# Fourteen filling tiles of the recurrent heads made in pairs, with seven half products a pair

## The chip, the cores and the metric

The kernel runs on one core of a Trainium2 chip. The metric is the device time of one launch in microseconds (us). Engines are PE (TensorE, matmuls), PEld (its weight loads), DVE (VectorE), ACT (ScalarE), POOL (GpSimd) and SP (SyncE, which here only issues DMAs).

## What is computed

The reference runs two transformer-like blocks over 512 tokens of width 1024, everything in float32. Only the first block's mixer matters here:

```python
h = _rmsnorm(x, norm_w[layer])
proj = jnp.einsum('bsd,de->bse', h, w_in[layer])          # ten slices of 1024 columns
(q_raw, ffwd_raw, fbwd_raw, i_raw, ga_raw,
 u_raw, v_raw, gb_raw, ma_raw, mb_raw) = jnp.split(proj, split_points, axis=-1)
y_a = _hgrn2_branch(q_raw, ffwd_raw, fbwd_raw, i_raw, ga_raw, ...)   # 8 recurrent heads, both directions
y_b = _spatial_gating_branch(u_raw, v_raw, gb_raw, ...)
```

The first five slices feed the eight recurrent heads. The slices u, v and gb (called g in the kernel) are wanted only by the stage after, the blend.

## The kernel before, in words

`gla_stage` holds the eight heads. A product of the projection is a "unit": one 128-column tile of weights against all 512 tokens, the contraction of 1024 in KT = 8 steps. A unit is a `project` (line 459): eight matmuls of 128 x 512, each with its own weight load, which the trace records as 16, two to a float32 matmul. Units go in turn to the two banks of `pj`; ACT copies each out (`evacuate`, line 580) before the bank is used again. 40 units ("p") belong to the heads, five a head, and are made one head ahead. 24 more ("v", "u", "g": `FILLS`) are filling: independent work put between the steps of a head, so that PE has something to do while DVE and ACT prepare the next step. Three of them open the stage, every head but the last takes two (`PER_HEAD`), and the last takes the remaining seven.

A head on PE (`attend`, and `attend_last` for the eighth) is an order written by hand: `turn_v`, two units, `turn_keys`, level 0, a unit, `chunk_sums`, level 1, `fill(0)`, level 2, a unit, levels 3 and 4, `fill(1)`, levels 5 to 7, a unit, `output`. A level is four 128 x 128 matmuls (line 485, eight records) on operands that DVE has scaled. On DVE the order is `operands`: for each level l it writes the exponents of level l + 1 (`level_log`, lines 742 to 745), scales the operands of level l by ACT's exponentials (`level_scale`, lines 753 to 756), and merges what PE made of level l - 2 (`merge`, lines 761 and 762). After level 4's step come `states` (lines 768 to 776) and the next head's `exponents`; after the levels come `log_sums` of the next head, the last merges and `scaled_q`. ACT's order is `decays` (the exponentials of line 616, one per level, with other work put after each by `prepare` or, in the last head, `closing`) and `out_norm`. Each engine runs its own instructions strictly in program order and waits at semaphores. `level(l)` waits for `level_scale(l)` and `merge(l - 2)`; `output` waits for all merges.

Weights lie in twelve slots of 512 KB. SP walks through the units in their order and reloads a slot when its unit is done (lines 427 to 438). The first weight tiles of the blend go to slots 4 to 9 as these come free (`BLEND_SLOTS`, line 439 on). The blend, the stage after, begins when all engines have ended the heads; it already makes its own products in pairs of tiles with the same seven half products (`product`, line 1018), with its sums of weights on DVE (lines 1243 to 1252) and its differences (line 1238).

Of the kernel before, what the change touches and what calls it, by code (L numbers as in the profile page):

```python
# [21 lines left out]
P = 128  # L22
# [39 lines left out]
for _name, _n in (("norm_w", 8), ("lb", 16), ("gnorm", 1), ("final", 8), ("mix", 8), ("pool_scale", 4),  # L62
# [8 lines left out]
FILLS = [("v", n) for n in range(4)] + [("u", 0), ("u", 1)] + [("v", n) for n in range(4, 8)] \  # L71
    + [("u", n) for n in range(2, 8)] + [("g", n) for n in range(8)]
OPENING = 3
PER_HEAD = 2
CLOSING = len(FILLS) - OPENING - PER_HEAD * (HEADS - 1)


def mixer_units():

    units = [("p", j) for j in range(QKV)] + FILLS[:OPENING]  # L80
    for i in range(HEADS - 1):
        p, f = [("p", QKV * (i + 1) + j) for j in range(QKV)], FILLS[OPENING + PER_HEAD * i:OPENING + PER_HEAD * (i + 1)]
        units += [p[0], p[1], p[2], f[0], p[3], f[1], p[4]]
    return units + FILLS[len(FILLS) - CLOSING:]

# [4 lines left out]
UG_SLOT = {("u", 0): (9, None), ("u", 1): (10, None), ("u", 2): (11, None), ("u", 3): (5, ("v", 7)), ("u", 4): (6, ("v", 7)),  # L90
# [3 lines left out]

BLEND_SLOTS = {4: ("p", QKV * HEADS - 1), 5: ("g", 2), 6: ("g", 3), 7: ("g", 4), 8: ("g", 5), 9: ("g", 6)}


def slot_value(unit):

    kind, n = unit  # L100
    if kind == "p":
        return 16 * (n // QKV + 1)
    if kind == "v":
        return 16 * (n // 4 + 1)
    slot, before = UG_SLOT[unit]
    if slot == 5:
        return 16 * (3 if before[0] == "v" else 4)
    return 16 if before is None or before[0] == "v" else 16 + slot_value(before)
# [247 lines left out]
def gla_stage(core, yaT, vg, uT, gT, raw, rs1):  # L356
# [12 lines left out]
    F_, B_, Q_, G_, V_ = range(QKV)  # L369
    scale = float(P) ** -0.5  # L370
    with ExitStack() as ctx:
# [28 lines left out]
        lnd = sb("log_diff", [P, 16])  # L400
        pj = ps("proj", [P, 2, 512])
# [3 lines left out]
        pS = ps("sum", [P, 512])  # L405
# [12 lines left out]
        h_ready = core.sem("h_ready")  # L418
        w0 = list(core.w_n)
        LEAD = 2  # L420

        with nc.Block() as block:
            @block.sync
            def _(sp):
                sp.dma_start(scan0[:], dram["scan_keep"][:]).then_inc(aux, 16)
                sp.dma_start(masks[:], dram["level_masks"][:]).then_inc(aux, 16)
                for n, (kind, m) in enumerate(UNITS):
                    if kind == "p" and m < QKV * (HEADS - 1):
                        sp.wait_ge(proj_done, n + 1)
                        j, i = m % QKV, m // QKV + 1  # L430
                        sp.dma_start(core.W[:, j, :], dram["w_gla"][i, :, j, :]).then_inc(core.w_in[j], 16)
                    if (kind, m) == ("v", 3):
                        sp.wait_ge(proj_done, n + 1)
                        sp.dma_start(core.wide(5, 4, 512), dram["w_v"][1]).then_inc(core.w_in[5], 16)
                    for (k2, m2), (slot, before) in UG_SLOT.items():
                        if before == (kind, m):
                            sp.wait_ge(proj_done, n + 1)
                            sp.dma_start(core.W[:, slot, :], dram["w_" + k2][m2]).then_inc(core.w_in[slot], 16)
                for slot in range(4, 4 + 2 * BLEND_RING):
                    sp.wait_ge(proj_done, UNIT_AT[BLEND_SLOTS[slot]] + 1)  # L440
                    blend_load(core, sp, slot - 4)

            def project(pe, unit, between=None):

                n, (kind, m) = UNIT_AT[unit], unit
                slot = m % QKV if kind == "p" else 5 if kind == "v" else UG_SLOT[unit][0]
                pe.wait_ge(core.w_in[slot], w0[slot] + slot_value(unit))
                if n >= 2:
                    pe.wait_ge(evac, n - 1)
# [12 lines left out]
            def turn_v(pe, i):  # L462
                pe.wait_ge(evac, UNIT_AT["p", i * QKV + V_] + 1)
                pe.wait_ge(st_ready, i + 1)
                for c in range(NB):
                    last = nc.tensor.transpose(pT[:, 0, c * P:(c + 1) * P], raw[:, V_, c * P:(c + 1) * P],
                                               core.ident[:])
                last.then_inc(vT_done, 1)

            def turn_keys(pe, i):  # L470
                pe.wait_ge(kd_ready, i + 1)
                pe.wait_ge(vn_ready, i + 1)
                for n in range(6):
# [38 lines left out]
            def square_sums(pe, i):  # L512
                pe.wait_ge(sq_done, i + 1)
                nc.tensor.matmul(pS[:], core.ones[:], sq[:], start=True, stop=True).then_inc(ss_done, 1)

            def attend(pe, i):
# [3 lines left out]
                def fill(n):  # L520
                    project(pe, FILLS[OPENING + PER_HEAD * i + n])
# [20 lines left out]
            def attend_last(pe, i):  # L542
                def fill(n, between=None):
                    project(pe, FILLS[len(FILLS) - CLOSING + n], between)

                turn_v(pe, i)
                fill(0, lambda: square_sums(pe, i - 1))
                fill(1)
# [15 lines left out]
                for n in range(7, CLOSING):  # L564
                    fill(n)
# [9 lines left out]
            def evacuate(act, unit):  # L575
                n, (kind, m) = UNIT_AT[unit], unit
                act.wait_ge(proj_done, n + 1)
                dst = {"p": lambda: raw[:, m % QKV], "v": lambda: vg[:, m % NB, m // NB * 512:m // NB * 512 + 512],
                       "u": lambda: uT[:, m], "g": lambda: gT[:, m]}[kind]()
                nc.scalar.copy(dst, pj[:, n % 2, :]).then_inc(evac, 1)  # L580

            def softplus(act, n, lo, chain):
# [3 lines left out]
                def first():  # L586
                    act.wait_ge(evac, UNIT_AT["p", (n - 1) * QKV + lo + 1] + 1)
# [23 lines left out]
            def decays(act, i, between):  # L611
                act.wait_ge(x_ready, i + 1)
                nc.scalar.activation(X[:], X[:], ACT.Exp).then_inc(ex_ready, 1)
                for l in range(LEVELS):
# [9 lines left out]
            def out_norm(act, i, chain):  # L624
# [3 lines left out]
                chain(nc.scalar.activation(rs[:], pS[:], ACT.Ln, bias=core.eps[:, 0:1], scale=1.0 / P))  # L628
# [3 lines left out]
            def _(act):  # L632
# [20 lines left out]
                for i in range(HEADS - 1):  # L653
# [3 lines left out]
                    def prepare(l):  # L657
# [3 lines left out]
                        if l in (1, 2, 3):  # L661
                            fb[l - 1]()
                        if l == 5:
                            evacuate(act, FILLS[OPENING + PER_HEAD * i])
# [7 lines left out]
                    evacuate(act, FILLS[OPENING + PER_HEAD * i + 1])  # L672
# [13 lines left out]
                evacuate(act, FILLS[len(FILLS) - CLOSING + 5])  # L686
                out_norm(act, HEADS - 1, chain)
                for unit in FILLS[len(FILLS) - CLOSING + 6:]:
                    evacuate(act, unit)
# [26 lines left out]

            def operands(dve, i, chain, previous, exponents_next, sums_next):

# [60 lines left out]
                level_log(0)  # L779
                if previous is not None:  # L780
                    previous()
                nc.vector.tensor_tensor(sg[:], raw[:, G_], ls[:, 3], ALU.mult)
                dve.wait_ge(ex_ready, i + 1)
                chain(nc.vector.tensor_copy(ed[:, 0], Xv[:, 0, :, P - 1]))
                chain(nc.vector.tensor_copy(ed[:, 1], Xv[:, 2, :, 0]))
                for n, (a, b) in enumerate(((qs[:], 0), (kk[:, 0], 1), (qs[:], 2), (kk[:, 1], 3))):
                    last = nc.vector.tensor_tensor(X[:, b], X[:, b], a, ALU.mult)
                last.then_inc(kd_ready, 1)
                dve.wait_ge(vT_done, i + 1)
                nc.vector.tensor_copy(vn[:].rearrange("p n c -> p (n c)"), pT[:, 0, :]).then_inc(vn_ready, 1)  # L790
                for l in range(LEVELS):
                    if l > 0:
                        dve.wait_ge(lv_ready, i * (LEVELS + 1) + l)
                    if l + 1 < LEVELS:
                        level_log(l + 1)
                    level_scale(l)
                    if l == LEVELS - 1:
                        dve.wait_ge(lv_ready, i * (LEVELS + 1) + LEVELS)
                        chain(nc.vector.tensor_copy(core.spare[:, 1:2], core.spare[:, 0:1]))
                        dve.engine_nop().then_inc(lv_ready, 1)  # L800
                    if l > 1:
                        merge(l - 2)
                    if l == 4:
                        states()
                        exponents_next()
                merge(LEVELS - 2)
                sums_next()
                for l in range(LEVELS - 1, LEVELS + 1):
                    merge(l)
# [10 lines left out]
            def _(dve):  # L820
# [34 lines left out]
                for i in range(1, HEADS - 1):  # L855
# [3 lines left out]
                    scaled_q(dve, i + 2)  # L859
                    chain.restart()  # L860
# [5 lines left out]
    for slot, times in zip(range(5, 12), (4, 2, 2, 2, 3, 3, 2)):  # L866
# [2499 lines left out]
def build(nc, dram, out):  # L3366
    with ExitStack() as ctx:
# [12 lines left out]
        with ExitStack() as first:  # L3380
# [3 lines left out]
            def opening(sp, free):  # L3384
                sp.dma_start(core.wide(5, 4, 512), dram["w_v"][0]).then_inc(core.w_in[5], 16)
                for n in range(3):
                    sp.dma_start(core.W[:, 9 + n, :], dram["w_u"][n]).then_inc(core.w_in[9 + n], 16)
# [157 lines left out]
```

## Time and profile before

| what | us |
|---|---|
| median of 3 runs (1501.77 to 1503.14) | 1503.04 |
| the profiled execution's own time | 1498.53 |
| its span in the trace | 1496.4 |
| PE busy in it | 1400.8 (94%) |
| DVE busy in it | 858.6 (57%) |
| ACT busy in it | 430.6 (29%) |
| mean granted TensorE clock | 0.983 of full |

The span is what the trace covers; the profiled execution's own time is 2.1 us longer. A row of the timeline gives start, length, engine, line, operation, what it writes and reads, the shape, a count, and in brackets how long the engine had been idle and what ended that. The length of a run of matmuls includes the end of the last one in the pipeline, so the next run starts a little before it; the pace is read from start to start.

### The profile page before, as it was taken

To read this page: it belongs to the slowest core of one execution; us is meant where nothing else is said; L and a number is where in the kernel's file an instruction comes from. 1 tells how busy PE (TensorE), PEld (TensorE's weight loads), DVE (VectorE), ACT (ScalarE), POOL (GpSimd) and SP (SyncE) were. 2 spreads that over 40 slices of the span, in tenths; PEclk is the share of its full clock that TensorE was granted. 3 is DMA by queue.
4 is the path that set the end of the run, shared out by engine and by line. 5 is a ranking of instruction groups with operands and counts; after the bars stand their busy time and mean duration, and the time that the engine had idled before them with its cause. 6 is when DMAs were issued, how large, how long until landed. Compare 5 with 4: busy or idle time off the path is not lost. (4 is left out here: it accounts for less than half of the span.)

```text
span 1496.4 us, 15038 instructions
## 1 busy us (share of the span) xinstructions
PE 1400.8 (94%) x5354; PEld 796.6 (53%) x5354; DVE 858.6 (57%) x1898; ACT 430.6 (29%) x706; POOL 57.5 (4%) x114
## 2 busy tenths in 40 slices
PE   7999999999999999999999999998899786899885
PEld 3455555555555558888888444445485433333222
DVE  5567677776777747867577349965573413222111
ACT  2435444444444415101112233134313330000000
POOL 0000000000000000000000000000000001122211
PEclk9999999999999999999999999999999996999998
DMA  7031111312210114223233122002213468999995
GB/s 290 29 113 57 42 57 30 111 57 57 70 42 15 43 57 169 85 68 103 88 139 135 38 84 71 15 9 85 77 65 147 152 265 341 400 409 405 407 409 164
DMA packets 38970, 201.97 MB, mean 135 GB/s; under 512 B 6896, under 2 KB 8816, under 8 KB 32112
## 3 DMA queue, kind: packets, MB, share of 16 engines
q1 hardware_dynamic: 31600, 186.29, 33.2%
q0 software_dynamic: 4608, 8.40, 2.3%
q10 hardware_dynamic: 2688, 6.29, 1.1%
q8 instruction: 46, 0.75, 0.2%
q14 instruction: 28, 0.23, 0.0%
HBM read 196.77 MB, written 12.58 MB: 140 GB/s over the span
## 5 line engine op out<-in xcount | busy, mean ns | idle before, releaser
L459 PE MATMUL gla_proj<-hT,weight_slots 128*128 128x512 f32 x864 | 379.5, 592 | 1.9 <-DVE hT L825 1.9
L459 PEld LDWEIGHTS gla_proj<-hT,weight_slots 128*128 128x128 f32 x864 | 160.8, 190 | 188.3 <-issue 187.6
L3102 PE MATMUL moe_banks<-weight_slots,moe_room 128*64 128x512 f32 x400 | 93.4, 616 | 14.3 <-DMA weight_slots<-in_w_gu 11.7
L1847 PE MATMUL mid_p_proj<-hT,weight_slots 128*128 128x512 f32 x208 | 93.0, 595 | 1.8 <-PEq L171 1.8
L3258 DVE SCALAR_TENSOR_TENSOR moe_room<-moe_banks,moe_kept,moe_room 128x256 f32<-128x256 f32 x16 | 7.7, 484 | 128.7 <-ACT moe_room L3213 128.7
L616 ACT ACTIVATE gla_level_decay<-gla_level_decay 128x1024 f32<-128x1024 f32 x56 | 58.9, 1055 | 46.0 <-DVE gla_level_decay L745 45.5
L1847 PEld LDWEIGHTS mid_p_proj<-hT,weight_slots 128*128 128x128 f32 x208 | 39.1, 190 | 52.1 <-issue 52.1
L3102 PEld LDWEIGHTS moe_banks<-weight_slots,moe_room 128*64 128x64 f32 x400 | 29.4, 141 | 69.9 <-issue 55.0
L485 PEld LDWEIGHTS gla_level<-gla_level_q,gla_level_k 128*128 128x128 f32 x448 | 55.0, 192 | 11.5 <-issue 11.5
L580 ACT COPY gla_raw<-gla_proj 128x512 f32<-128x512 f32 x38 | 22.4, 590 | 122.9 <-PE gla_proj L459 122.9
L485 PE MATMUL gla_level<-gla_level_q,gla_level_k 128*128 128x128 f32 x448 | 56.3, 275 | 0.0
L459 PE MATMUL gla_proj<-weight_slots,hT 128*128 128x512 f32 x128 | 55.9, 592 | 0.0
L3213 ACT ACTIVATE moe_room<-moe_banks,moe_kept 128x256 f32<-128x256 f32 x16 | 7.6, 474 | 160.1 <-PE moe_banks L3102 160.1
L761 DVE COPY spare<-spare 128x1 f32<-128x1 f32 x64 | 9.5, 149 | 71.8 <-PE gla_level L485 71.3
L2800 POOL DMA_INDIRECT ex_rows<-h_rows,ix_rows x1 | 1.2, 1196 | 1248.4 <-issue 1248.4
L762 DVE COPY_PREDICATED gla_scores<-gla_level_masks,gla_level 128x512 f32<-128x512 int32 x64 | 46.8, 731 | 2.2
L3127 PE MATMUL moe_banks<-weight_slots,moe_room 128*64 128x512 f32 x176 | 41.7, 619 | 4.1 <-issue 4.1
L459 PEld LDWEIGHTS gla_proj<-weight_slots,hT 128*128 128x128 f32 x128 | 23.9, 190 | 28.2 <-issue 28.2
L3268 DVE COPY moe_room<-moe_banks 128x512 f32<-128x512 f32 x16 | 11.1, 692 | 48.6 <-PE moe_banks L3127 48.6
L2514 DVE CUSTOM_DVE_ANT_0 sa_probs<-sa_S,qkT_bias 128x512 f32<-128x512 f32 (+3 forms) x32 | 14.4, 489 | 39.8 <-PE sa_S L2317 39.8
L753 DVE TENSOR_TENSOR gla_level_q<-gla_q,gla_level_decay 128x256 f32<-128x256 f32 x56 | 23.4, 417 | 16.2 <-ACT gla_level_decay L616 16.2
L1018 PE MATMUL bl_p_x<-hT,weight_slots 128*128 128x256 f32 x128 | 30.0, 380 | 1.9 <-PEq L171 1.9
(503 smaller groups left out, 2483.3 us busy)
## 6 DMA issues: line engine op xcount, KB each, us to landing
weight_slots<-in_w_gu SPq DMA_DIRECT2D x25, 2048.0 KB, 22.0
weight_slots<-in_w_gla SPq DMA_DIRECT2D x40, 512.0 KB, 3.6
weight_slots<-in_w_dn SPq DMA_DIRECT2D x10, 2048.0 KB, 28.0
weight_slots<-in_w_merge SPq DMA_DIRECT2D x32, 512.0 KB, 4.2
weight_slots<-in_w_out SPq DMA_DIRECT2D x16, 512.0 KB, 4.5
weight_slots<-in_w_v SPq DMA_DIRECT2D x3, 2048.0 KB, 7.5
hT<-in_w_gu SPq DMA_DIRECT2D x3, 2048.0 KB, 36.0
weight_slots<-in_w_u SPq DMA_DIRECT2D x8, 512.0 KB, 5.6
```

The costliest lines, as they stand in the source:

```text
L459: last = nc.tensor.matmul(pj[:, n % 2, :], lhsT, rhs, start=(k == 0), stop=(k == KT - 1))
L485: last = nc.tensor.matmul(pA[:, l % 2, c * P:(c + 1) * P], k, q, start=True, stop=True)
L580: nc.scalar.copy(dst, pj[:, n % 2, :]).then_inc(evac, 1)
L616: nc.scalar.activation(Tl[:, l % 2], Tl[:, l % 2], ACT.Exp).then_inc(e_ready, 1)
L753: nc.vector.tensor_tensor(side(QL[:, l % RING], 0), side(qs[:], 0), side(Tl[:, l % 2, 1], 0), ALU.mult)
L762: nc.vector.copy_predicated(A[:], masks[:, l].unsqueeze(1).to_broadcast([P, NB, P]), pA[:, l % 2].rearrange("p (n t) -> p n t", t=P)).then ...
L1018: ins = nc.tensor.matmul(bank, b[:, k * P:(k + 1) * P], a[:, k, :], start=first and k == 0, stop=(k == H - 1), skip_group_check=not first)
L1847: last = nc.tensor.matmul(pw[:, n % 2, :], a, b, start=(k == 0), stop=(k == KT - 1))
L2514: last = nc.vector.tensor_tensor_reduce(pr[:, i % RINGP, hh, 0:w], pS[:, i % 2, hh, 0:w], bias[:, b, 0:w], 1.0, -3.0e38, ALU.add, ALU.max, ...
L3102: last = nc.tensor.matmul(pG[rows, e, :], hgT[:, k, rows], core.as_gate_up(at[k // 4])[:, x, k % 4, :], start=(k == 0), stop=(k == KT - 1))
L3127: last = nc.tensor.matmul(pY[rows, half, :], hidT[:, e, f * P + CAP * x:f * P + CAP * x + CAP], core.as_down(at)[:, x, f, half * 512:half ...
L3268: nc.vector.tensor_copy(ys[:, e, 512:1024], pY[:, 1, :]).then_inc(yb, 1)
```

## The change

The tiles u1 to u7 and g0 to g6 are made two at a time. Written as 2 x 2 blocks of half the contraction by 128 columns of weights (b11, b21 from the first tile, b12, b22 from the second) and half the contraction by 256 tokens of hT, the eight half products of a pair become seven, each four matmuls of 128 x 256. "x" of a pair (`pair_opens`) makes x first, z first, x second, z second; "y" (`pair_closes`) makes y first, z third, y second. Heads 3 to 6 take one pair each, x at `fill(0)` and y at `fill(1)`. The last takes three pairs and g7. The four combinations of hT (`form`) are made once, into slots 5 to 8; four sums of weights (`weight_sums`) and five differences (`second`, `third`, `rest_22`, `rest_21`, `rest_12`) are made on DVE for each pair, two copies on ACT in place of two. The bank `pZ` takes the place of `pS`, which now is half of `pT`. Slots 9 and 10 carry the pairs, one after another (the sixth pair is in slots 11 and 4), and the blend's slots 5 to 9 are loaded after ("y", 6).

```diff
+FIRST_PAIRED = 3
+PAIRED = [(("u", 1), ("u", 2)), (("u", 3), ("u", 4)), (("u", 5), ("u", 6)), (("u", 7), ("g", 0)), (("g", 1), ("g", 2)),
+          (("g", 3), ("g", 4)), (("g", 5), ("g", 6))]
+PAIR_SLOTS = [(9, 10)] * 5 + [(11, 4), (9, 10)]
-BLEND_SLOTS = {4: ("p", QKV * HEADS - 1), 5: ("g", 2), 6: ("g", 3), 7: ("g", 4), 8: ("g", 5), 9: ("g", 6)}
+BLEND_SLOTS = {4: ("y", 5), 5: ("y", 6), 6: ("y", 6), 7: ("y", 6), 8: ("y", 6), 9: ("y", 6)}
...
+            def product(bank, b, a, first, between=None):
+                for k in range(H):
+                    if k == 1 and between is not None:
+                        between()
+                    ins = nc.tensor.matmul(bank, b[:, k * P:(k + 1) * P], a[:, k, :], start=first and k == 0,
+                                           stop=(k == H - 1), skip_group_check=not first)
+                return ins
+            def pair_opens(pe, n, between=None):
...
+                product(bank, b11(n), hT[:, 0:H, 0:Q], True, between).then_inc(xa_done, 1)
+                pe.wait_ge(formed, 2)
+                pe.wait_ge(summed, 4 * n + 2)
+                if n:
+                    pe.wait_ge(c21_out, n)
+                product(pZ[:, 0:Q], sums[:, 1], forms[:, 1], True).then_inc(z1_done, 1)
+                pe.wait_ge(x1_out, n + 1)
+                product(bank, b21(n), hT[:, H:KT, 0:Q], False).then_inc(proj_done, 1)
...
+                pe.wait_ge(u2_out, n + 1)
+                product(pZ[:, 0:Q], b12(n), forms[:, 2], False).then_inc(z2_done, 1)
+            def z_third(pe, n):
+                pe.wait_ge(summed, 4 * n + 4)
+                pe.wait_ge(u3_out, n + 1)
...
+            def y_second(pe, n):
+                pe.wait_ge(formed, 4)
+                pe.wait_ge(c22_out, n + 1)
...
             def attend_last(pe, i):
                 turn_v(pe, i)
-                fill(0, lambda: square_sums(pe, i - 1))
-                fill(1)
+                pair_opens(pe, 4, lambda: square_sums(pe, i - 1))
+                pair_closes(pe, 4)
                 turn_keys(pe, i)
                 level(pe, i, 0)
                 chunk_sums(pe, i)
-                fill(2)
+                pair_opens(pe, 5)
                 level(pe, i, 1)
+                pair_closes(pe, 5)
                 level(pe, i, 2)
-                fill(3)
                 level(pe, i, 3)
+                pair_opens(pe, 6)
                 level(pe, i, 4)
-                fill(4)
-                for l in range(5, LEVELS + 1):
-                    level(pe, i, l)
-                fill(5)
+                y_first(pe, 6)
+                level(pe, i, 5)
+                z_third(pe, 6)
+                level(pe, i, 6)
+                y_second(pe, 6)
+                level(pe, i, 7)
                 output(pe, i)
-                fill(6, lambda: square_sums(pe, i))
-                for n in range(7, CLOSING):
-                    fill(n)
+                project(pe, LAST_PLAIN, lambda: square_sums(pe, i))
...
                 def closing(l):
-                    if l in (0, 1, 3, 5, 6):
-                        evacuate(act, FILLS[len(FILLS) - CLOSING + (0, 1, 3, 5, 6).index(l)])
+                    if l == 1:
+                        x_first_out(act, 5)
+                    if l == 2:
+                        evacuate(act, ("x", 5))
+                    if l == 4:
+                        x_first_out(act, 6)
+                    if l == 5:
+                        evacuate(act, ("x", 6))
...
+            def weight_sums(dve, n):
...
+                nc.vector.tensor_tensor(sums[:, 0], b11(n), b12(n), ALU.add).then_inc(summed, 1)
+                dve.wait_ge(summed, 4 * n + 1)
+                nc.vector.tensor_tensor(sums[:, 1], sums[:, 0], b22(n), ALU.add).then_inc(summed, 1)
...
                 for l in range(LEVELS):
                     if l > 0:
                         dve.wait_ge(lv_ready, i * (LEVELS + 1) + l)
                     if l + 1 < LEVELS:
                         level_log(l + 1)
+                    if n == 0 and l == 2:
+                        form(dve, 2)
+                    if last_head and l == 2:
+                        second(dve, 5)
                     level_scale(l)
+                    if last_head and l == 0:
+                        rest_12(dve, 4)
+                        weight_sums(dve, 5)
...
+                    if n == 0 and l == 3:
+                        form(dve, 3)
+                    if n == -1 and l == 4:
+                        weight_sums(dve, 0)
+                    if paired and l == 4:
+                        second(dve, n)
+                        third(dve, n)
+                    if last_head and l == 3:
+                        third(dve, 5)
+                    if last_head and l == 4:
+                        rest_22(dve, 5)
+                    if last_head and l == 5:
+                        rest_12(dve, 5)
+                    if last_head and l == 6:
+                        second(dve, 6)
                     if l > 1:
                         merge(l - 2)
                     if l == 4:
                         states()
                         exponents_next()
+                    if paired and l == 5:
+                        rest_22(dve, n)
+                    if last_head and l == 4:
+                        rest_21(dve, 5)
+                    if last_head and l == 5:
+                        weight_sums(dve, 6)
```

What the diff above leaves out: in heads 3 to 6 DVE makes `rest_21` and `rest_12` after the levels, before `merge` 5, and the next pair's `weight_sums` after `scaled_q`; at the end of head 2 it makes `form` 0 and 1. ACT makes `x_first_out` after the exponential of level 4 and no copy for y. In the last head DVE makes `second` 4 after the first `level_log`, `third` 4 before it waits for ACT's edge exponentials, `rest_22` and `rest_21` 4 around the copy of v, `third` and `rest_22` 6 after the levels; ACT makes `x_first_out` 4 and `evacuate` ("x", 4) around the edge exponentials, before the first level's. `turn_keys` also waits for `rs_done` of the head before.

## Rows read from the trace of the kernel before

**Rows 1.** The page: busy time of each engine over the whole span.
```profile
PE 1400.8 (94%) x5354; PEld 796.6 (53%) x5354; DVE 858.6 (57%) x1898; ACT 430.6 (29%) x706; POOL 57.5 (4%) x114
```

**Rows 2.** Stretches (head 4, last): length; PE, PEld, DVE, ACT, POOL busy; PEclk; DMA.
```profile
313.90:375.68 61.78, 61.24 (x222) 33.42 (x221) 46.13 (x108) 27.14 (x32) 0.00 (x0) 1.00 0.21 60
499.25:561.87 62.62, 62.36 (x224) 33.69 (x222) 38.31 (x100) 16.79 (x22) 0.00 (x0) 1.00 0.14 44
```

**Rows 3.** Timeline of PE, head 4.
```profile
339.58 7.03 PE L459 MATMUL gla_proj<-hT,weight_slots 128*128 128x512 f32 x16
346.45 1.05 PE L485 MATMUL gla_level<-gla_level_q,gla_level_k 128*128 128x128 f32 x8
...
365.99 7.03 PE L459 MATMUL gla_proj<-hT,weight_slots 128*128 128x512 f32 x16
373.35 0.49 PE L503 MATMUL gla_out<-gla_scores,gla_v 128*128 128x128 f32 x2 [0.33 <-DVE gla_scores L762]
```

**Rows 4.** Timeline of PE at the start of the blend.
```profile
568.98 1.89 PE L1018 MATMUL bl_p_z<-bl_h_forms,bl_w_sums 128*128 128x256 f32 x8
570.70 1.89 PE L1018 MATMUL bl_p_y<-hT,bl_w_sums 128*128 128x256 f32 x8
```

**Rows 5.** Timeline of DVE at the start of the blend: a form, a difference, a sum.
```profile
566.24 1.22 DVE L1238 TENSOR_TENSOR bl_h_forms<-hT 128x1024 f32<-128x1024 f32 x1
...
571.01 0.41 DVE L1238 TENSOR_TENSOR bl_second<-bl_first,bl_p_z 128x256 f32<-128x256 f32 x1
571.34 0.68 DVE L1243 TENSOR_TENSOR bl_w_sums<-weight_slots 128x512 f32<-128x512 f32 x1
```

**Rows 6.** Timeline of DVE, head 4.
```profile
340.60 0.41 DVE L742 TENSOR_TENSOR gla_level_decay<-gla_cum 128x256 f32<-128x256 f32 x1
...
342.94 0.41 DVE L756 TENSOR_TENSOR gla_level_k<-gla_keys,gla_level_decay 128x256 f32<-128x256 f32 x1
347.54 0.15 DVE L761 COPY spare<-spare 128x1 f32<-128x1 f32 x1 [4.19 <-PE gla_level L485]
...
357.49 0.74 DVE L762 COPY_PREDICATED gla_scores<-gla_level_masks,gla_level 128x512 f32<-128x512 int32 x1
...
375.88 0.43 DVE L725 COPY gla_edge<-gla_cum 128x512 f32<-128x512 f32 x1 [2.02 <-PE gla_out L505]
```

**Rows 7.** Timeline of ACT: two rows of head 4, one of the blend.
```profile
338.99 1.05 ACT L616 ACTIVATE gla_level_decay<-gla_level_decay 128x1024 f32<-128x1024 f32 x1
...
363.06 0.59 ACT L580 COPY xT<-gla_proj 128x512 f32<-128x512 f32 x1 [2.79 <-PE gla_proj L459]
...
565.72 0.37 ACT L1147 COPY bl_first<-bl_p_x 128x256 f32<-128x256 f32 x1 [3.23 <-PE bl_p_x L1018]
```

**Rows 8.** Timeline of PE, last head.
```profile
524.36 1.95 PE L485 MATMUL gla_level<-gla_level_q,gla_level_k 128*128 128x128 f32 x16
```

**Rows 9.** Timeline of DVE, last head.
```profile
525.45 0.15 DVE L761 COPY spare<-spare 128x1 f32<-128x1 f32 x1 [3.06 <-PE gla_level L485]
...
529.75 0.28 DVE L768 COPY gla_states<-gla_turned 128x128 f32<-128x128 f32 x1
...
531.80 0.42 DVE L742 TENSOR_TENSOR gla_level_decay<-gla_cum 128x256 f32<-128x256 f32 x1
```

**Rows 10.** Busy time by stretch, late stage (columns as in rows 2).
```profile
1304.00:1308.00 4.00, 3.93 (x14) 2.34 (x16) 1.36 (x3) 0.00 (x0) 0.00 (x0) 0.50 1.02 396
1308.00:1312.00 4.00, 4.00 (x18) 1.14 (x16) 0.81 (x2) 0.59 (x1) 0.23 (x2) 0.87 1.04 438
```

**Rows 11.** Timeline of PE, late stages.
```profile
1145.56 3.67 PE L2099 MATMUL cr_p_q<-hT,weight_slots 128*128 128x512 f32 x8 [2.08 <-PEq L1541]
...
1304.07 1.97 PE L3089 MATMUL moe_banks<-ident,ex_rows 128*128 128x128 f32 x8 [4.15 <-DMA ex_rows<-h_rows,ex_ix]
...
1420.53 5.35 PE L3102 MATMUL moe_banks<-weight_slots,moe_room 128*64 128x512 f32 x16 [2.10 <-DMA weight_slots<-in_w_gu]
```

**Rows 12.** DMA issues, 360 to 376 us: size in KB, us to landing.
```profile
weight_slots<-in_w_gla SPq DMA_DIRECT2D x1, 512.0 KB, 3.6
```

More of the change, by code:

```diff
@@ L104, in slot_value @@
         return 16 * (n // 4 + 1)
[L105 to L108, printed above, removed]
+    return 16 if unit == ("u", 0) else 48
 PLACES = 11
@@ L400, in gla_stage @@
         lnd = sb("log_diff", [P, 16])
+        sums = sb("w_sums", [P, 3, H * P])
+        forms = flat(core.W[:, 5:9, :]).rearrange("p (n k t) -> p n k t", n=4, t=Q)
         pj = ps("proj", [P, 2, 512])
@@ L404, in gla_stage @@
         pO = ps("out", [P, 512])
-        pS = ps("sum", [P, 512])
+        pZ = ps("pair", [P, 512])
+        pS = pT[:, 1, :]
         aux = core.sem("aux_loaded")
@@ L434, in _ @@
                         sp.dma_start(core.wide(5, 4, 512), dram["w_v"][1]).then_inc(core.w_in[5], 16)
[L435 to L438, printed above, removed]
+                    if (kind, m) in (("u", 0), ("p", QKV * HEADS - 1)):
+                        sp.wait_ge(proj_done, n + 1)
+                        pair_load(sp, 5, int(kind == "p"))
+                    if kind == "y" and m < len(PAIRED) - 1:
+                        sp.wait_ge(proj_done, n + 1)
+                        if m == 5:
+                            sp.dma_start(core.W[:, 11, :], dram["w_g"][7]).then_inc(core.w_in[11], 16)
+                        else:
+                            for x in range(2):
+                                pair_load(sp, m + 1 if m < 4 else 6, x)
                 for slot in range(4, 4 + 2 * BLEND_RING):
@@ L577, in evacuate @@
                 act.wait_ge(proj_done, n + 1)
+                if kind == "x":
+                    nc.scalar.copy(part(m, 0, 0), pj[:, n % 2, 0:Q]).then_inc(evac, 1)
+                    return
                 dst = {"p": lambda: raw[:, m % QKV], "v": lambda: vg[:, m % NB, m // NB * 512:m // NB * 512 + 512],
@@ new lines, in form, with second @@
+            def form(dve, n):
+                if n == 0:
+                    dve.wait_ge(proj_done, UNIT_AT["v", 7] + 1)
+                    sub(forms[:, 0], hT[:, 0:H, Q:T], hT[:, H:KT, Q:T]).then_inc(formed, 1)
+                    return
+                dve.wait_ge(formed, min(n, 2))
+                a, b = ((hT[:, 0:H, 0:Q], forms[:, 0]), (hT[:, H:KT, Q:T], forms[:, 1]), (hT[:, H:KT, 0:Q], forms[:, 1]))[n - 1]
+                sub(forms[:, n], a, b).then_inc(formed, 1)
+            def second(dve, n):
+                dve.wait_ge(x1_out, n + 1)
+                dve.wait_ge(z1_done, n + 1)
+                sub(part(n, 0, 1), part(n, 1, 0), pZ[:, 0:Q]).then_inc(u2_out, 1)
@@ new lines, in third, with rest_22, rest_21 @@
+            def third(dve, n):
+                dve.wait_ge(z2_done, n + 1)
+                sub(part(n, 1, 1), part(n, 1, 0), pZ[:, 0:Q]).then_inc(u3_out, 1)
+            def rest_22(dve, n):
+                dve.wait_ge(y1_done, n + 1)
+                dve.wait_ge(u3_out, n + 1)
+                sub(part(n, 1, 1), pj[:, UNIT_AT["y", n] % 2, 0:Q], part(n, 1, 1)).then_inc(c22_out, 1)
+            def rest_21(dve, n):
+                dve.wait_ge(z3_done, n + 1)
+                sub(part(n, 1, 0), part(n, 1, 0), pZ[:, 0:Q]).then_inc(c21_out, 1)
@@ L717, in operands, with rest_12 @@
+            def rest_12(dve, n):
+                dve.wait_ge(proj_done, UNIT_AT["y", n] + 1)
+                dve.wait_ge(u2_out, n + 1)
+                sub(part(n, 0, 1), pj[:, UNIT_AT["y", n] % 2, 0:Q], part(n, 0, 1)).then_inc(c12_out, 1)
             def operands(dve, i, chain, previous, exponents_next, sums_next):
+                n, last_head = i - FIRST_PAIRED, i == HEADS - 1
+                paired = n >= 0 and not last_head
                 if previous is not None:
@@ L805, in operands @@
                         exponents_next()
+                    if paired and l == 5:
[4 more added lines that the diff above has]
+                        weight_sums(dve, 6)
+                if paired:
+                    rest_21(dve, n)
+                    rest_12(dve, n)
+                if last_head:
+                    third(dve, 6)
+                    rest_22(dve, 6)
                 merge(LEVELS - 2)
                 sums_next()
-                for l in range(LEVELS - 1, LEVELS + 1):
-                    merge(l)
+                if last_head:
+                    rest_21(dve, 6)
+                merge(LEVELS - 1)
+                if last_head:
+                    rest_12(dve, 6)
+                merge(LEVELS)
             def result(dve, i, chain, h):
@@ L865, in gla_stage @@
         core.w_n[j] += 16 * HEADS
-    for slot, times in zip(range(5, 12), (4, 2, 2, 2, 3, 3, 2)):
+    for slot, times in zip((4, 5, 9, 10, 11), (1, 2, 6, 6, 3)):
         core.w_n[slot] += 16 * times
```

139 lines of the change are left out of this document (114 added, 25 removed), and 3 rows, old and new, of the table UG_SLOT.

## The prediction

> **What bounds the kernel now.** I read the page first: PE is busy for 94% of the span [rows 1]. Then the eight heads, where the change lies: in head 4 PE is busy for 61.24 of 61.78 us at full clock while DVE is busy for 46.1, in the last head for 62.36 of 62.62 with DVE at 38.3 [rows 2]. So PE sets the length of a head and what shortens its matmuls shortens the kernel, as long as DVE's and ACT's new work fits their idle time at the right moment. Third, the timelines, for when each engine reaches each step.
>
> **PE's saving.** A unit takes 6.87 us, start to start (339.58 to 346.45), and the next starts at once [rows 3]. A pair is now two units, 13.73 us. Each of the seven half products is eight records of 128 x 256, which the blend makes in 1.72 us, start to start [rows 4]; seven are 12.04 us. A pair saves 1.7 us: "x" takes 6.9, as the unit it replaces, "y" 5.15. Seven pairs would give 12 us if nothing waited.
>
> Against this speaks a rule. The blend's row shows 24 more weight loads a pair (56 for 32) at no cost: its records stand exactly half as far apart as those of 512 columns [rows 3, 4]. The Trainium skill ("TensorE: Matmul & The Clock Gate", Back-to-back issue gap) says that the spacing in a stream of loads and matmuls is set by both, and that at few columns the matmul's own time counts too little; its "LDWEIGHTS" section gives 107 ns a load. By an estimate from that page, 24 exposed loads would cost 2.6 us a pair and make each pair 0.9 us slower.
>
> **New work on DVE and ACT.** A weight sum takes 0.6 to 0.7 us, a difference 0.35 to 0.4, a form 1.2 [rows 5]; per pair four sums (2.6 us) and five differences (1.8 us). ACT copies 256 columns in 0.37 instead of 512 in 0.59 [rows 7]. The bound for the new waits on pZ comes from the same rows: it is the blend's own operation.
>
> **Heads 3 to 6: the work fits.** Head 4, in the times of before. x first starts at 339.58 [rows 3], ends at 341.3, z first at 343.0. ACT has ended the exponential of level 4 at 340.0 [rows 7] and copies x first by 341.9, 1.1 us before x second wants it. DVE ends level 4's scaling at 343.3 [rows 6] and makes `second` by 343.7; z second wants it at 344.7. `third` waits for z second until 346.7, inside the 4.2 us in which DVE stood idle for level 2 [rows 6]. y first starts where `fill(1)` did, 6.87 us before its end at 362.86 (ACT's copy follows at 363.06 [rows 7]), so at 356.0, and z third ends at 359.4; DVE ends merge 3 at 358.2 [rows 6] and `rest_22` by 358.6, so y second has some 0.6 us to spare, the tightest place. `weight_sums` of the next pair (2.5 us) falls where DVE waits for `output` (2.0 us [rows 6], and more now). Its two loads are issued nearly ten microseconds earlier, against 3.6 us to landing [rows 12]. The forms go into head 2's end (2.4 us against 2.0 idle; PE asks for DVE's work there only at `turn_keys`, two units or 13.7 us later) and into idle time of head 3, the first pair's sums into level 4's wait of head 2: nothing.
>
> There is a second gain. Now ACT can start the next head's log-sigmoid only after copying `fill(1)` at 363.06 [rows 7], and DVE's `log_sums` and last merges follow from it; PE's `output` starts at 373.35 instead of 372.86, with a slow first step, some 0.55 us in all [rows 3]. y needs no copy by ACT, so this chain starts 3 us earlier and the wait goes. Per head 1.7 + 0.55 = 2.3 us, four heads: 9.2 us saved.
>
> **The last head: the work does not fit.** Three pairs come in one head, and the order on DVE is fixed. A level costs DVE 2.7 us (`level_log` and `level_scale`, 340.60 to 343.3 [rows 6]), a merge 0.8, `states` 2.05 (529.75 to 531.80 [rows 9]), two levels on PE 1.78 (524.36 + 1.95, less the overlap of 0.17 [rows 8]). Counting us from `turn_v`, and each engine in its order:
> - y second of pair 4 wants `rest_22` at 11.6, DVE has it at 12.0: 0.4 wait.
> - Level 0 wants its operands at 14.4. DVE has them at 15.6, since two differences, a wait for z second and `rest_21` stand before: 1.2.
> - z third of pair 5 wants `third` at 27.4, it ends at 28.1 after level 3's scaling: 0.8.
> - y second of pair 5 wants `rest_22` at 29.9, but it stands behind level_log 5, scaling 4 and merge 1: 31.9. Wait 2.1.
> - Levels 2 and 3 end at 35.5, x first of pair 6 at 37.2. z first then wants `weight_sums(6)`. DVE had been waiting for level 2 (34.6) and has, in order, merge 2 (0.85), `states` with its waits (2.2), `rest_21`, level_log 6 and scaling 5 (2.7), `rest_12`, merge 3 (0.85) and two sums (1.4): they are there at 43.5. Wait **6.3**.
> - x second ends at 46.95. ACT's exponential of level 6 stands behind its copy of x, so it ends at 48.5; scaling 6 (1.4) and `second(6)` follow: z second starts at 50.6. Wait 3.7.
> - At the end `third`, `rest_22`, `rest_21` and `rest_12` stand between the merges, and `output` waits 1.2.
>
> Together 15.7 us of waits, less three savings of 1.7 and the 0.4 that PE waits there now: the last head becomes 10.1 us longer. The same working for the kernel of before gives 61.8 us for a head and 62.2 for the last, against 61.8 and 62.6 read [rows 2].
>
> **The clock.** In these heads the granted clock is 1.0, 2.4 GHz [rows 2]. After an idle 4.15 us in a late stage it was 0.5 (1.2 GHz) for the 4 us that follow and 0.87 over the next 4 [rows 10, 11], about 2.5 us lost; after one of 2.10 us sixteen records took 5.35 us, which at 0.22 each would be 3.5, about 1.8 lost; after another of 2.08 us nothing was lost (eight took 3.67, at 0.43 each 3.4 and the end of the last) [rows 11]. The waits of 6.3 and 3.7 us are of the kind that loses it, and z first and x second of pair 6 between them are on the chain. Bounds: 0 (clock held) and 5 us (both falls in full). I take 2.7: one fall in full, as after the 4.15 us, and little of the second.
>
> **After the head.** y6 ends 12 us before the blend can begin (level 7, `output`, g7 and the 1.85 us of the stage's end), so the five loads behind it land in time at 3.6 us the first: nothing, at most 2 us if they queue.
>
> **Sum.** -9.2 + 10.1 + 2.7 = +3.6 us, on the profiled execution's 1498.53 us: 1502.1. That execution lies 4.5 us under the median; I put the same +3.6 on the median, 1503.04, and get 1506.6. From no change this kernel's measurement can tell about 0.2%, 3.0 us.
>
> **Rivals.**
> 1. The clock holds or hardly falls: +0.9 us, 1503.9. For it: waits of 2 us passed without loss [rows 11]. Against: 6.3 us is three times as long.
> 2. DVE gets ahead in the last head. If its idle 3.1 us before merge 1 [rows 9] and the rest absorb the work, and `weight_sums(6)` is there when z first wants it, the last head saves its 5.2 us: -9.2 - 5.2 = -14.4, 1488.7; with half of the waits (7.8 us) -6.5, 1496.5. It decides on whether the two sums are there before x first ends, at 37.2. Against: the sums stand after merge 3 in DVE's program, and merge 3 after level 3 on PE, so at least 2.2 us must pass where x first covers 1.7, before `states` and level 6 are counted.
> 3. The pairs stall in heads 3 to 6 as well, at y second, where 0.6 us is spare, or at `second`: from 0.6 us of lateness on it costs. If DVE is 2.1 us later than I have it (three differences and a merge that I have placed wrongly), 1.5 us show in each of four heads, +6: +9.6, 1512.6. For it: the margin is thin. Against: DVE's steps there are read, not assumed [rows 6].
> 4. The loads of weights are exposed (the page's rule as a mechanism of this kernel): the blend's half product would have to take longer here than its 1.72 us. A record of a level, 128 columns and a load, takes 0.11 us (16 in 1.78 [rows 8]); if each of the 24 extra loads showed that much, it costs 2.6 us a pair, 18 us in seven: +22, 1525. The blend's rows speak against it outright [rows 4].
>
> **Chances.** Forecast (waits as worked out, with a fall of the clock) 0.54, between +1.5 and +6.5. Rival 1: 0.12. Rival 2: 0.14, nearly all in its weaker form. Rival 3: 0.18. Rival 4: 0.02. Faster by over 0.2% is rival 2, 0.14. Slower by over 0.2% is rivals 3 and 4 and over half of the forecast's case, 0.50. The rest, 0.36, is within 0.2%: rival 1 and the lower part of the forecast. The range leaves out the strong end of rival 2 and the outer part of rival 3: 1498.5 to 1512.0.
>
> **What would show it.** In the profile after: head starts (`turn_v`) 59.5 us apart from head 3 on; rows of the product's line in the heads, 32 records of 128 x 256 in x, in 6.9 us; PE's wait for DVE's weight sums before the first product of pair 6, near 6 us, and one of over 3 us for the difference after it; the granted clock under 1 in the last 35 us of the heads; last head near 75 us. I am wrong if the last head is under 66 us, if PE waits at the pairs of heads 3 to 6, or if a half product there takes over 1.8 us.

## The result, and the profile after

The changed kernel takes 1504.95 us (median of 11 runs, 1502.26 to 1508.16) against 1502.13 (11 runs of before). The ratio is 1.0023, with a 95% interval of 1.0013 to 1.0034: by this ratio 3.5 us slower, between 2 and 5 (the two medians alone are 2.8 us apart). The forecast was +3.6 us; as a time it was 1506.6, put on the earlier median of 1503.04. In the profiled execution, 1504.95 us:

```profile
span 1503.2 us, 15499 instructions
PE 1395.2 (93%) x5522; PEld 831.0 (55%) x5522; DVE 894.0 (59%) x1965; ACT 427.5 (28%) x706; POOL 57.3 (4%) x114
```

PE is busy for 5.6 us less than in [rows 1] and DVE for 35 us more, and the whole is longer. So PE has less to do and stands more. Where it stands is shown by the busy time of the changed kernel in two stretches, head 6 but for its first 0.45 us, and the last head up to the blend's first product (length; PE, PEld, DVE, ACT, POOL busy; granted clock; DMA share; GB/s):

```profile
431.00:490.09 59.09, 58.87 (x242) 37.60 (x241) 50.29 (x117) 26.46 (x32) 0.00 (x0) 1.00 0.07 24
490.09:568.32 78.23, 62.21 (x296) 49.48 (x295) 48.81 (x124) 16.05 (x23) 0.00 (x0) 0.93 0.18 65
```

Head 6 is as full as head 4 was before [rows 2], with DVE at 50.3 us instead of 46.1. The last head has 16 us in which PE does nothing, and a granted clock of 0.93. The starts of heads 3, 4, 5 and 6 (`turn_v`, timeline of PE) stand 59.54 us apart, where they were 61.78 before:

```profile
251.91 0.60 PE L573 MATMUL gla_turned<-ident,gla_raw 128*128 128x128 f32 x4
311.46 0.60 PE L573 MATMUL gla_turned<-ident,gla_raw 128*128 128x128 f32 x4
371.00 0.60 PE L573 MATMUL gla_turned<-ident,gla_raw 128*128 128x128 f32 x4
430.55 0.60 PE L573 MATMUL gla_turned<-ident,gla_raw 128*128 128x128 f32 x4
```

The last head begins at 490.09 instead of 499.25: 9.2 us gained. The blend begins at 568.32 instead of 563.72, 4.6 us late. So the last head takes 78.2 us instead of 64.5, and gives back 13.8. (0.2 of the 9.2 us is no gain of the pairs: the changed kernel's first head already starts at 67.42 instead of 67.62.) This is where (timeline of PE, last head, after):

```profile
502.30 1.97 PE L507 MATMUL gla_proj<-weight_slots 128*128 128x256 f32 x8 [0.30 <-DVE weight_slots L848]
...
505.82 1.16 PE L594 MATMUL gla_level<-gla_level_q,gla_level_k 128*128 128x128 f32 x8 [0.90 <-DVE gla_level_k L938]
...
518.41 1.97 PE L507 MATMUL gla_pair<-hT,gla_w_sums 128*128 128x256 f32 x8 [0.56 <-DVE weight_slots L848]
522.23 1.97 PE L507 MATMUL gla_proj<-weight_slots 128*128 128x256 f32 x8 [1.85 <-DVE weight_slots L848]
524.03 1.95 PE L594 MATMUL gla_level<-gla_level_q,gla_level_k 128*128 128x128 f32 x16
525.81 1.89 PE L507 MATMUL gla_proj<-hT,weight_slots 128*128 128x256 f32 x8
533.63 3.75 PE L507 MATMUL gla_pair<-weight_slots,gla_w_sums 128*128 128x256 f32 x8 [5.93 <-DVE gla_w_sums L858]
537.18 1.98 PE L507 MATMUL gla_proj<-hT,weight_slots 128*128 128x256 f32 x8
542.92 2.54 PE L507 MATMUL gla_pair<-weight_slots 128*128 128x256 f32 x8 [3.77 <-DVE weight_slots L848]
545.26 1.91 PE L594 MATMUL gla_level<-gla_level_q,gla_level_k 128*128 128x128 f32 x8
...
556.30 0.49 PE L612 MATMUL gla_out<-gla_scores,gla_v 128*128 128x128 f32 x2 [1.00 <-DVE gla_scores L944]
```

These are the seven waits of the prediction, in its order and at its places: 0.3, 0.9, 0.56, 1.85, 5.93, 3.77, 1.0, together 14.3 us. The brackets count from the modelled end of the last matmul, the prediction from when the next one would have started. Counted its way (at z first of pair 6 from 525.81 + 1.73 to 533.63: 6.1 us) the seven are 0.5, 1.1, 0.7, 2.0, 6.1, 3.9 and 1.2, together 15.5 where 15.7 were forecast. After the longest, z first of pair 6 takes 3.55 us from start to start, not 1.73. The granted clock has fallen to 0.50, its lower level of 1.2 GHz, and it falls again after the next wait, of 3.77 us (stretches of z first of pair 6 and of level 4, columns as above):

```profile
533.63:537.18 3.55, 3.55 (x9) 2.83 (x9) 1.11 (x2) 0.00 (x0) 0.00 (x0) 0.50 0.02 5
545.26:546.97 1.71, 1.71 (x9) 1.71 (x8) 0.00 (x0) 0.00 (x0) 0.00 (x0) 0.50 0.00 0
```

What DVE does in PE's 5.9 us (timeline of DVE, after):

```profile
525.12 0.15 DVE L943 COPY spare<-spare 128x1 f32<-128x1 f32 x1 [3.04 <-PE gla_level L594]
...
527.99 0.41 DVE L848 TENSOR_TENSOR weight_slots<-weight_slots,gla_pair 128x256 f32<-128x256 f32 x1
528.32 0.42 DVE L924 TENSOR_TENSOR gla_level_decay<-gla_cum 128x256 f32<-128x256 f32 x1
...
531.51 0.72 DVE L944 COPY_PREDICATED gla_scores<-gla_level_masks,gla_level 128x512 f32<-128x512 int32 x1
532.13 0.68 DVE L856 TENSOR_TENSOR gla_w_sums<-weight_slots 128x512 f32<-128x512 f32 x1
532.84 0.69 DVE L858 TENSOR_TENSOR gla_w_sums<-gla_w_sums,weight_slots 128x512 f32<-128x512 f32 x1
...
540.62 0.43 DVE L935 TENSOR_TENSOR gla_level_q<-gla_q,gla_level_decay 128x256 f32<-128x256 f32 x1 [5.88 <-ACT gla_level_decay L738]
```

DVE first stands idle for 3.0 us, waiting for level 2; then come merge 2, the states, `rest_21`, level 6's exponents, level 5's scaling, `rest_12`, merge 3, and only then the two sums that PE wants. The last row is the cause of the 3.8 us: DVE waits 5.9 us for ACT's exponential of level 6. In the timeline of ACT:

```profile
528.01 1.06 ACT L738 ACTIVATE gla_level_decay<-gla_level_decay 128x1024 f32<-128x1024 f32 x1
539.19 0.37 ACT L692 COPY weight_slots<-gla_proj 128x256 f32<-128x256 f32 x1 [10.12 <-PE gla_proj L507]
539.46 1.06 ACT L738 ACTIVATE gla_level_decay<-gla_level_decay 128x1024 f32<-128x1024 f32 x1
```

ACT stood for 10.1 us at its copy of x, with the exponential queued behind it.

### The profile page after: what moved, and what is told of

It reads as the page before. It is cut to its first block and busy times, and to the rows that moved or that the text cites. A ratio compares the mean times of both kernels' runs of the same rounds, so it can differ in the third digit from the quotient of the medians.

```text
span 1503.2 us, 15499 instructions
## 1 busy us (share of the span) xinstructions
PE 1395.2 (93%) x5522; PEld 831.0 (55%) x5522; DVE 894.0 (59%) x1965; ACT 427.5 (28%) x706; POOL 57.3 (4%) x114
## 5 line engine op out<-in xcount | busy, mean ns | idle before, releaser
L566 PE MATMUL gla_proj<-hT,weight_slots 128*128 128x512 f32 x640 | 281.0, 592 | 1.9 <-DVE hT L1053 1.9
L566 PEld LDWEIGHTS gla_proj<-hT,weight_slots 128*128 128x128 f32 x640 | 119.2, 190 | 141.0 <-issue 140.2
```

Source lines behind the costliest of these rows:

```text
L566: last = nc.tensor.matmul(pj[:, n % 2, :], lhsT, rhs, start=(k == 0), stop=(k == KT - 1))
```

## The experiments

In each of them the length of the last head is taken from `turn_v` to the blend's first product, in one profiled execution. Each ratio is to runs of the kernel before that were made beside it. The changed kernel (1.0023) was not run again beside the experiments, so a difference from it in ratio goes over two such comparisons.

**1. The sums earlier.** One move on DVE in the last head.

```diff
                     if last_head and l == 4:
                         rest_22(dve, 5)
+                        weight_sums(dve, 6)
...
-                    if last_head and l == 5:
-                        weight_sums(dve, 6)
```

> One edit on the changed kernel: in the last head DVE makes weight_sums(6) straight after rest_22(5), in the 3.0 us in which it waits for level 2, not behind merge 3. Theory (the order on DVE makes PE's wait of 5.9 us): that wait falls to at most 1.2 us (z first then waits for rest_21(5), which still stands behind states), the clock does not fall there, and the last head, 78.2 us from turn_v to the blend's first product, becomes 70 to 71.5 us; against the kernel of before about -3 us, ratio 0.998. The wait of 3.8 us for second(6) stays, since ACT's copy of x and the exponential of level 6 still stand before it. Rival (DVE simply has too much work in this head, wherever it stands): the wait only moves, to level 4 or to the next product, and the last head stays over 76 us, ratio over 1.001.

Measured: ratio 0.9990 (0.9979 to 1.0001), last head 71.30 us (489.96 to 561.26), granted clock in it 0.98. Timeline of PE of this experiment:

```profile
528.40 1.97 PE L507 MATMUL gla_pair<-weight_slots,gla_w_sums 128*128 128x256 f32 x8 [0.84 <-DVE weight_slots L848]
...
535.86 2.72 PE L507 MATMUL gla_pair<-weight_slots 128*128 128x256 f32 x8 [3.77 <-DVE weight_slots L848]
```

The wait of 5.93 us has become 0.84, now for `rest_21(5)`, and z first of pair 6 runs at full pace. The wait of 3.77 us is unchanged and now it alone is followed by a lower clock (0.70 granted from 535.86 to 538.50). The last head is 6.9 us shorter than in the changed kernel. The rival, that DVE has too much work wherever it stands, falls: DVE had idle time at the place to which the sums were moved. By the traces this experiment shows it; its ratio holds 1.000.

**2. PE kept at work in its two long waits.**

```diff
+            def warm(pe, count):
+                pe.wait_ge(y_done, HEADS)
+                for k in range(count):
+                    nc.tensor.matmul(pO[:], core.ones[:], hT[:, k, :], start=True, stop=True)
...
+                if n == 6:
+                    warm(pe, 6)
                 pe.wait_ge(formed, 2)
                 pe.wait_ge(summed, 4 * n + 2)
...
+                if n == 6:
+                    warm(pe, 3)
                 pe.wait_ge(formed, 3)
```

> One edit on the changed kernel: before its two long waits in pair 6 PE makes dummy products of 128 x 512 into the idle bank of the output, six (5.2 us) in the wait of 5.9 us and three (2.6 us) in that of 3.8 us. The order and the waits of DVE and ACT are untouched. Theory (the lost clock costs some 3.6 us on top of the waits): granted clock 1.00 throughout the heads, z first of pair 6 back from 3.55 to 1.73 us, last head 78.2 -> 74.5 to 75 us, ratio to before about 1.000. Rival (the clock is no cost of its own, since DVE and ACT set the pace after these waits anyway): clock back at 1.00 but the last head within 1 us of 78.2, ratio 1.002.

The dummy products go to the bank of the output, which is idle then. Measured: ratio 1.0007 (0.9995 to 1.0019), last head 74.74 us. Timeline of PE, and the stretch of the last head, of this experiment:

```profile
528.01 5.31 PE L514 MATMUL gla_out<-hT,ones 128*128 128x512 f32 x12
534.11 1.97 PE L507 MATMUL gla_pair<-weight_slots,gla_w_sums 128*128 128x256 f32 x8 [0.79 <-issue]
...
537.64 2.74 PE L514 MATMUL gla_out<-hT,ones 128*128 128x512 f32 x6
541.57 1.97 PE L507 MATMUL gla_pair<-weight_slots 128*128 128x256 f32 x8 [1.19 <-DVE weight_slots L857]
```
```profile
490.57:565.31 74.74, 66.44 (x314) 50.19 (x313) 48.80 (x124) 16.05 (x23) 0.00 (x0) 1.00 0.20 69
```

PE does more work than in the changed kernel and the stretch is 3.5 us shorter, at a granted clock of 1.00. The waits themselves are as they were: z first begins 6.1 us after x first has ended (528.01 to 534.11), as in the changed kernel (527.5 to 533.63). (The row's "issue" names no releaser; DVE's second sum ends at 534.00, just before.) The rival, that the clock costs nothing since DVE and ACT set the pace, falls in the trace; the ratio alone, whose interval holds 1.000 and overlaps that of the changed kernel, would not decide it. So of the 13.8 us that the last head lost, 3.5 are the clock and 10.3 the waits less the saving. The changed kernel's own rows give 3.6: z first and x second of pair 6 are 1.9 us longer than at full clock, z second 0.6, level 4 0.8 and y first 0.3.

**3. The last head plain.** Pairs in heads 3 to 6 alone; g1 to g7 in the last head in the order of before, with their weights in slots of their own as these come free.

```diff
-LAST_PLAIN = ("g", 7)
+LAST = [("g", n) for n in range(1, 8)]
+LAST_SLOTS = {1: (9, ("y", 3), 5), 2: (10, ("y", 3), 5), 3: (11, ("u", 0), 2), 4: (5, ("y", 3), 3), 5: (6, ("y", 3), 1), 6: (7, ("y", 3), 1),
+              7: (10, ("g", 2), 6)}
```

> The change without its last head: pairs in heads 3 to 6 alone, the last head with seven plain tiles (g1 to g7) in the order of before. Theory (the gain of the pairs in heads 3 to 6 is 9.2 us and whole, all that is lost is in the last head): last head 64.5 us as before, kernel -9.2 us, ratio 0.9939. Rival (the earlier start is partly given back later, at loads of the blend or in the last stages): ratio over 0.996.

Measured: ratio 0.9936 (0.9919 to 0.9952), -9.6 us. The last head runs from 490.89 to 555.22, 64.3 us. PE's waits from head 3 to the blend, all of them (engine, line, for whom, total us, times, longest):

```profile
PE bl_p_x L1206 <- PEq L189: 1.7, 1, 1.7
PE gla_level L592 <- DVE gla_scores L931: 1.1, 5, 0.2
```

The wait before `output` is gone in heads 3 to 6. Their gain is whole, and by the runs nothing after it takes it back. All that the change lost it lost in the last head.

**4. Two more moves.** On the first experiment, `rest_21(5)` before merge 2 too, and `second(6)` before the scaling of level 6.

```diff
                         weight_sums(dve, 6)
+                        rest_21(dve, 5)
...
+                    if last_head and l == 6:
+                        second(dve, 6)
                     level_scale(l)
...
-                    if last_head and l == 6:
-                        second(dve, 6)
```

> On the first experiment, two more moves on DVE in the last head: rest_21(5) also before merge 2, and second(6) before the scaling of level 6 (so not behind ACT's exponential of level 6). Theory (each wait has one cause, the order): waits before z first of pair 6 gone, before z second of pair 6 from 3.8 to about 1.5 us, clock 1.00 in the heads, last head 66 to 66.5 us, against before -7.4 us, ratio 0.995. Rival (DVE's whole load binds): last head over 70 us.

Measured: ratio 0.9958 (0.9943 to 0.9972), last head 66.16 us (490.46 to 556.62). Timeline of PE of this experiment:

```profile
527.90 1.89 PE L507 MATMUL gla_pair<-weight_slots,gla_w_sums 128*128 128x256 f32 x8
532.72 1.97 PE L507 MATMUL gla_pair<-weight_slots 128*128 128x256 f32 x8 [1.20 <-DVE weight_slots L848]
```

The two waits of 9.7 us together are 1.2, by three moves of instructions that DVE makes in any case. With all seven pairs the kernel is now 6.3 us faster than before. In the traces its last head is still 1.8 us longer than in the third experiment, 66.16 against 64.33, though the intervals of the two ratios overlap: the remaining waits of this head (0.3, 0.9, 0.56, 1.85, 1.2, 1.0) are more than its three pairs save (5.2 us).

**5. One pair in the last head, where DVE is idle.** Heads 3 to 6 as in the change; in the last head g1 to g4 and g7 plain, the pair (g5, g6) with x after level 4 and y after level 7.

```diff
                 level(pe, i, 4)
+                pair_opens(pe, 4)
                 for l in range(5, LEVELS + 1):
                     level(pe, i, l)
+                pair_closes(pe, 4)
                 output(pe, i)
...
+                if last_head:
+                    second(dve, 4)
+                    third(dve, 4)
                 merge(LEVELS - 2)
...
                 merge(LEVELS)
+                if last_head:
+                    rest_22(dve, 4)
+                    rest_21(dve, 4)
+                    rest_12(dve, 4)
```

> Pairs in heads 3 to 6, and in the last head one pair alone, (g5, g6), where the trace shows DVE idle: x after level 4, y after level 7 and before the output; g1 to g4 and g7 are plain tiles. Its differences stand before merge 5 (DVE idle for 4.9 us there) and after the last merge. Theory (a pair saves 1.7 us wherever DVE reaches its steps in time): no wait of PE over 0.3 us in the last head, 62.6 to 63.0 us from turn_v to the blend's first product against 64.5, ratio to before 0.9927 (-10.9 us), 1.7 us less than with the last head plain. Rival (the last pair ends too near the end of the stage: the blend's weights in slots 5 to 9 are loaded only after it, or the differences after the last merge are late): PE waits at y second or at the blend's start, last head 64.5 us or more, ratio 0.994.

Measured: ratio 0.9931 (0.9916 to 0.9946), -10.4 us, the lowest ratio of all versions. The last head is 62.68 us. Timeline of PE of this experiment:

```profile
535.54 1.13 PE L591 MATMUL gla_level<-gla_q,gla_level_k 128*128 128x128 f32 x8 [0.21 <-DVE gla_scores L932]
536.51 1.89 PE L504 MATMUL gla_proj<-weight_slots,gla_w_sums 128*128 128x256 f32 x8
538.24 1.89 PE L504 MATMUL gla_pair<-hT,gla_w_sums 128*128 128x256 f32 x8
539.96 1.89 PE L504 MATMUL gla_proj<-weight_slots 128*128 128x256 f32 x8
541.69 0.38 PE L609 MATMUL gla_out<-gla_scores,gla_v 128*128 128x128 f32 x2
...
553.61 5.42 PE L1214 MATMUL bl_p_x<-hT,weight_slots 128*128 128x256 f32 x24 [1.70 <-PEq L188]
```

No wait between the products, none at the blend's start beyond its usual 1.7 us. The traces give 1.65 us less for the last head than with it plain; the two ratios (0.9936, 0.9931) are too close for the runs to tell them apart.

**6. The margin in heads 3 to 6.**

```diff
-                    if paired and l == 5:
-                        rest_22(dve, n)
...
+                    if paired and l == 6:
+                        rest_22(dve, n)
```

> One edit on the changed kernel: in heads 3 to 6 DVE makes rest_22 only after the scaling of level 6, about 1.6 us later; the last head is left as it is. This measures the margin that my third rival was about. Theory (y second has 0.6 to 0.9 us to spare in these heads, read from DVE's difference, ended at 415.7, and y second, begun at 416.6): PE waits 0.7 to 1.1 us at y second in each of the four heads, heads 60.3 to 60.6 us apart instead of 59.54, kernel +3 to +4.4 us on the changed one, ratio to before 1.0045 to 1.005. Rival (the delay is taken up by the waits that follow on levels 5 to 7, which PE had anyway): heads within 0.3 us of 59.54, ratio 1.0023.

Measured: ratio 1.0049 (1.0033 to 1.0065), heads 60.6 us apart. Timeline of PE of this experiment:

```profile
312.35 0.60 PE L573 MATMUL gla_turned<-ident,gla_raw 128*128 128x128 f32 x4
...
358.92 1.97 PE L507 MATMUL gla_proj<-weight_slots 128*128 128x256 f32 x8 [0.82 <-DVE xT L848]
...
372.96 0.60 PE L573 MATMUL gla_turned<-ident,gla_raw 128*128 128x128 f32 x4
```

`rest_22` in the changed kernel (head 5, timeline of DVE), and in this experiment (head 4):

```profile
415.26 0.41 DVE L848 TENSOR_TENSOR xT<-gla_proj,xT 128x256 f32<-128x256 f32 x1
```
```profile
358.35 0.42 DVE L848 TENSOR_TENSOR xT<-gla_proj,xT 128x256 f32<-128x256 f32 x1
```

Counted from y first (413.13 and 354.49) it begins 2.1 and 3.9 us in, a delay of 1.7 us. It costs PE 0.82 us of waiting and 1.06 us of each head. In the changed kernel the difference ends at 415.67 and y second begins at 416.59; here 0.15 us lie between the two (358.77 to 358.92). So y second has nearly 0.8 us to spare where 0.6 were forecast, and the other 1.0 of the 1.7 us is paid in full: my third rival was a real mechanism, some 0.8 us away from costing anything.

## Why the prediction was right, point by point

- **Seven half products at 1.72 us.** Right: 398.41 to 400.14 is one of many. The third experiment gives the whole gain of four heads, so the weight loads are not exposed. The fourth rival is refuted in these heads as in the blend. So is the estimate of 2.6 us more a pair from the Trainium skill ("TensorE: Matmul & The Clock Gate", Back-to-back issue gap and LDWEIGHTS).
- **Heads 3 to 6.** -9.2 forecast; from head 3's start to the last head's it is 238.18 us instead of 247.13, so -8.95. Per head 2.24: the pair's 1.7 and the 0.55 of the wait before the output, which is gone (481.0 + 6.87 = 487.86, the output's start). The prediction had rounded the same two terms up to 2.3.
- **The waits of the last head.** +10.1 forecast; with the clock held it is 74.74 - 64.47 = +10.3. Each wait was found at its place, within 0.3 us counted the prediction's way, and z first of pair 6 starts 43.54 us into the head for 43.5 forecast. The moves of the first and fourth experiments show that the order on DVE is the cause of the two long ones, and the fourth that ACT's copy matters only as long as `second(6)` stands behind the exponential. For the other five, 5.5 us of the 15.5, the cause is read from the timelines; no run moved a step for one of them.
- **The clock.** +2.7 forecast, 3.5 measured (78.23 against 74.74). The step was right in kind and its split was wrong: I had put 2.5 us on the first fall and 0.2 on the second. The first cost 1.9. The second cost 1.7: z second takes 2.34 us, level 4 1.71 and y first 2.03 after it, instead of 1.73, 0.9 and 1.73. Part of the one error hid the other.
- **After the head.** Nothing, as forecast: the blend's loads behind y6 cost no wait. From the blend's first product to the next stage's the time is the same, 269.98 us before (563.72 to 833.70) and after (568.32 to 838.30).
- **The sum.** At the blend's start +4.6 in the traces for +3.6 (+4.8 without the 0.2 us by which the first head began earlier): the clock 0.8 over the forecast, heads 3 to 6 and the waits 0.2 each. Over all runs it is +3.5, between 2 and 5, so that this meets +3.6 to 0.1 us is luck. The spans of the two profiled executions differ by 6.8 us, 4.6 in the heads and 2.2 in stages whose code is the same. The profiled execution of before, 1498.53 us at a mean clock of 0.983, is below all eleven runs of the result; runs of the unchanged kernel beside the experiments went from 1497.0 (clock 0.986) to 1504.7 us (0.978 to 0.980). That these 2.2 us are no effect of the change is likely but only argued: in the third experiment, too, 6.3 of the 8.5 us gained by then are missing at the end of its profiled execution, while its median shows the whole gain.
- **The signs.** The last head was forecast near 75 us. That was counted, as in [rows 2], without the wait ahead of the blend's first product, and by this count it is 76.5.
- **The rivals.** The first (clock holds) is refuted by the half product of 3.55 us, the second (DVE gets ahead) by the 5.93 us wait, the third by the heads 59.54 us apart without a wait at a pair.

```profile
398.41 1.89 PE L507 MATMUL gla_pair<-weight_slots,gla_w_sums 128*128 128x256 f32 x8
400.14 1.89 PE L507 MATMUL gla_proj<-hT,weight_slots 128*128 128x256 f32 x8
```
```profile
480.99 7.03 PE L566 MATMUL gla_proj<-hT,weight_slots 128*128 128x512 f32 x16
487.86 0.38 PE L612 MATMUL gla_out<-gla_scores,gla_v 128*128 128x128 f32 x2
```

## What to carry to other kernels

A saving on the busiest engine is worth its full size only where the helper's new steps are done before the busy engine wants them: here the same pair saved 2.2 us a head in four heads and cost 4.6 us apiece, three of them, in the last, mostly by its place in a fixed order. Write down, for each new wait, what stands before the awaited instruction in its engine's program and when that can run; it told the places and sizes of seven waits beforehand to within 0.3 us. If such a wait cannot be avoided on TensorE, its price includes the granted clock afterwards, 3.5 us for two waits of 9.7 us here.

## What the runs showed of the hardware that I had not expected

In the first experiment one wait of 3.77 us alone was followed by a lower granted clock: the half product after it took 2.5 us instead of 1.73. The wait of 1.85 us in the same head was not. And PE at work on dummy products held the clock at 1.00 over the same two gaps, and delayed nothing in the trace (z first and z second of pair 6 begin 6.1 and 3.9 us after the product before has ended, with and without them). In the traces the last head is 3.5 us shorter. By the ratios the kernel is about 2.4 us faster (1.0023 to 1.0007), but these intervals overlap, so the runs alone don't show it.
